# A two-block model on one core: fills of the first attention spread by work, conditioning chunks moved, dense products of the recurrence in halves

## The reference

```python
for l in range(2):
    mod, mod_c = silu(c) @ w_ada[l] + b_ada[l], silu(c_ctx) @ w_ada[l] + b_ada[l]   # 3072 columns: shift, scale, gate
    if l == 0:   # x 512 rows, ctx 256 rows
        q, k, v, g_a, xb, b_g, c_g, g_b = split(modulate(x) @ w_in_ab)        # and the same for ctx
        o_a = window_attention(rope(q), rope(k), v, kc, vc, sink)              # 8 heads, 2 key heads, |s-t| <= 128
        o_b = b_g * short_conv(c_g * xb, conv_w)                               # three taps
        y = concat(o_a * silu(g_a), o_b * silu(g_b)) @ w_out_ab
        x = layer_norm(alpha * x + gate * y); ctx likewise
    else:
        q, zf, zb, i, g = split(modulate(x) @ w_in_c); ctx: zf, zb, i
        # per head and direction: k = 1 - f(z), S_t = diag(f_t) S_{t-1} + k_t v_t, o_t = S_t q_t
        # ctx first gives the starting state; forward and backward are added
        y = (rms(o_f + o_b) * g_norm * silu(g)) @ w_out_c
        x = layer_norm(alpha * x + gate * y)
```

## Time and profile before

| | |
|---|---|
| median of 3 runs | 2454.27 us (2452.99 to 2455.32) |
| profiled execution, its own time | 2457.86 us |
| its span | 2456.1 us |
| mean granted TensorE clock over it | 0.948 |
| first attention's stretch | 209.70 to 463.85 us |
| recurrence's stretch | 609.60 to 1130.80 us |

### The profile page before, as it was taken

The page is one execution under the profiler, slowest core; times in us unless marked ns, Lnnn a source line. Parts: engine busy times, 40 slices in busy tenths (PEclk is TensorE's granted clock), DMA queues, the critical chain, the costliest instruction groups (busy, mean ns, idle before and its releaser), DMA issues. The chain is left out here.

```text
span 2456.1 us, 27907 instructions
## 1 busy us (share of the span) xinstructions
PE 2243.3 (91%) x11655; PEld 1798.7 (73%) x11655; DVE 1104.9 (45%) x1647; ACT 668.0 (27%) x1030; POOL 835.7 (34%) x393
## 2 busy tenths in 40 slices
PE   5989996978999999999798878999998999999998
PEld 3768885856676767787665667888887767888886
DVE  2023557652556556556996553111116783111113
ACT  3222223223444444453111333010003163010111
POOL 1322102410323323223800024554554345454553
PEclk7999997979999999999899988999999999999999
DMA  9321115351101011112121012332322222232322
GB/s 296 83 72 52 35 35 172 79 163 52 35 23 47 18 35 35 35 52 78 42 65 35 35 35 70 102 103 86 103 92 97 86 86 69 86 103 88 101 95 77
DMA packets 173212, 187.45 MB, mean 76 GB/s; under 512 B 25552, under 2 KB 151840, under 8 KB 172960
## 3 DMA queue, kind: packets, MB, share of 16 engines
q1 hardware_dynamic: 165520, 178.56, 23.1%
q10 hardware_dynamic: 6992, 5.01, 0.7%
q0 software_dynamic: 576, 2.10, 0.2%
HBM read 183.56 MB, written 2.10 MB: 76 GB/s over the span
## 5 line engine op out<-in xcount | busy, mean ns | idle before, releaser
L2816 POOL TENSOR_TENSOR weights_lo<-weights_raw,weights_hi 128x2048 fp32r<-128x2048 f32 (+1 forms) x104 | 471.0, 4528 | 849.5 <-ACT weights_hi L1334 637.6
L646 PE MATMUL ring<-input_hi,weights_hi 128*128 128x512 f32 x784 | 305.4, 390 | 0.0
L648 PE MATMUL ring<-input_hi,weights_lo 128*128 128x512 f32 x784 | 305.0, 389 | 0.0
L647 PE MATMUL ring<-input_lo,weights_hi 128*128 128x512 f32 x784 | 305.0, 389 | 0.0
L2653 DVE CAST weights_hi<-weights_raw 128x2048 fp32r<-128x2048 f32 (+1 forms) x72 | 88.8, 1233 | 378.6 <-PE ring L648 173.9
L2807 POOL TENSOR_TENSOR h_w<-h_p 128x512 f32<-128x512 f32 x56 | 70.3, 1256 | 448.1 <-PE ring L935 367.6
L908 PE MATMUL obank<-acts,weights_raw 128*128 128x512 f32 x384 | 175.2, 611 | 0.8 <-issue 0.8
L646 PEld LDWEIGHTS ring<-input_hi,weights_hi 128*128 128x128 f32 x784 | 147.2, 188 | 31.1 <-issue 0.5
L648 PEld LDWEIGHTS ring<-input_hi,weights_lo 128*128 128x128 f32 x784 | 147.2, 188 | 30.6
L647 PEld LDWEIGHTS ring<-input_lo,weights_hi 128*128 128x128 f32 x784 | 147.2, 188 | 30.5 <-issue 0.2
L919 PE MATMUL obank<-weights_raw,acts 128*128 128x256 f32 x640 | 145.4, 387 | 0.0
(11 more groups left out here) (457 smaller groups left out, 4459.2 us busy)
## 6 DMA issues: line engine op xcount, KB each, us to landing
weights_raw<-in_w_ada SPq DMA_DIRECT2D x24, 1024.0 KB, 7.2
weights_raw<-in_ffn_w_gate SPq DMA_DIRECT2D x22, 1024.0 KB, 5.2
weights_raw<-in_ffn_w_up SPq DMA_DIRECT2D x22, 1024.0 KB, 5.2
weights_raw<-in_w_in_c SPq DMA_DIRECT2D x20, 1024.0 KB, 5.1
weights_raw<-in_ffn_w_down SPq DMA_DIRECT2D x16, 1024.0 KB, 4.9
weights_raw<-in_w_in_ab SPq DMA_DIRECT2D x9, 1024.0 KB, 5.2
weights_raw<-in_ev_w_in SPq DMA_DIRECT2D x8, 1024.0 KB, 5.8
weights_raw<-in_od_w_in SPq DMA_DIRECT2D x8, 1024.0 KB, 5.8
```

Source lines behind the costliest of these rows:

```text
L646: pe.matmul(o, hi[:, k, ms], xh[:, k, t0:t0 + n], start=k == 0, stop=False)
L647: pe.matmul(o, hi[:, k, ms], xl[:, k, t0:t0 + n], start=False, stop=False)
L648: last = pe.matmul(o, lo[:, k, ms], xh[:, k, t0:t0 + n], start=False, stop=k == KD - 1)
L2816: pool.tensor_tensor(W_LO[slot][:, 0:kt, :], WR[:, slot, 0:kt, :], w_hi[:, 0:kt, :], ALU.subtract).then_inc(sem("w_lo"), 1)
```

## The change

It does the following, all in the first block.

1. **Fills by work.** A list `a_woven` of all units is spread over 24 even places by cost (`fill_cost`, in matmuls); a place may hold several units.
2. **Conditioning.** Sixteen chunks (`MODS`): five stand behind `kv`, `ga0`, `ga1`, `gb0` and `gb1`, one each; seven are fills; four, (1,8) to (1,11), stand between the first dense products of the recurrence.
3. **Gate rows** of layer 0 are fills; that of layer 1 comes behind the first part of i.
4. **Late high parts.** ScalarE rounds the weights of y0.1 and later at the third tile of the y before it, y0.0 at the unit cg1.1.0, yc0.2 and yc0.3 on either side of LayerNorm's root. Convolution parts run behind the units of cg. x is loaded again from ScalarE's queue in four column pieces.
5. **Turned tiles of layer 1** (`h1.0` to `h1.3`) stand right behind yc0.3, `h1.4` and `h1.5` behind the second part of z. A chunk's slot is given back after its last part, in the order in which chunks were taken.
6. **Recurrence.** Dense products are cut in halves (`product_half`) and spread over the places. The diagonal is made once for a pair of heads, in the backward step, from the sum of both directions' keys (`keys_of_both`). `exclusive` on GpSimd is gone: backward scans on VectorE give the exclusive sums. The first two level operands stand ahead of the diagonal, the query operand behind the first scores.

```diff
-            return units + [None] * (8 - len(units))
+            halves = [unit + (half,) for unit in units for half in range(2)]
+            if st == LAST:
+                share = (2, 2, 2, 2, 2, 0, 0, 0)
+            else:
+                share = (2, 2, 2, 1, 1, 1, 1, 0) if len(units) == 5 else (2, 2, 2, 1, 2, 1, 2, 0)
+            at = [sum(share[:i]) for i in range(9)]
+            return [halves[at[i]:at[i + 1]] for i in range(8)]
...
+        MODS_AHEAD, MODS_LATE = 5, 4
+        a_woven, mods_left = [], list(range(MODS_AHEAD, len(MODS) - MODS_LATE))
+        for nm, c, x, m in AB_UNITS:
+            a_woven.append((nm, c, x, m))
+            if (nm, c, x) == ("cg", 1, 1):
+                a_woven += [("x_again",)] * m + [("y_hi", 2 * m), ("y_hi", 2 * m + 1)]
+            elif (x, m) == (1, 1):
+                a_woven.append(("mod", mods_left.pop(0)))
+            if nm == "bg":
+                a_woven += {(0, 0, 0): [("gate_diag", 0)], (0, 0, 1): [("gate", 0)],
+                            (0, 1, 0): [("gate_diag", 1)], (0, 1, 1): [("gate", 1)]}.get((c, x, m), [])
+        for unit in Y_UNITS[:-3]:
+            a_woven.append(unit)
+            if unit[2] == TL - 1 and mods_left:
+                a_woven.append(("mod", mods_left.pop(0)))
+            if unit == ("y", 2, TL - 1):
+                a_woven += [("ctx_again",), ("last_mod",)]
+        assert not mods_left
+
+        def fill_cost(unit):
+
...
+            return 2 * KD if unit[0] in ("mod", "gate") else 3 * KD * (2 if unit[0] != "y" and unit[2] == 0 else 1)
+
+        A_PLACES = 24
+        a_costs = [fill_cost(u) for u in a_woven]
         AB_FILL = {}
-        for u, unit in enumerate(AB_UNITS):
-            AB_FILL[u * AB_STEPS // len(AB_UNITS)] = unit
-        MOD_FIRST = 6
...
-        Y_WOVEN = 48 - AB_STEPS - MOD_FIRST
-        for u in range(Y_WOVEN):
-            AB_FILL[AB_STEPS + MOD_FIRST + u] = Y_UNITS[u]
-        Y_AFTER = Y_UNITS[Y_WOVEN:]
+        for u, unit in enumerate(a_woven):
+            place = min(A_PLACES - 1, A_PLACES * (2 * sum(a_costs[:u]) + a_costs[u]) // (2 * sum(a_costs)))
+            AB_FILL.setdefault(2 * place, []).append(unit)
         mod_no = {}
...
+            def mod_next(s):
+
+                if s:
+                    mod_turn(*MODS[s - 1])
+                mod_rows(*MODS[s])
+
...
-            mod_run(1, MOD_FIRST, 12)
+            for t in range(TL):
+                pe.wait_ge(sem("x1_ready"), t + 1)
+                turn_tiles("h1.", X, (t,), "va"[t % 2])
...
-            for t in range(6):
-                pe.wait_ge(sem("x1_ready"), t + 1)
-                turn_tiles("h1.", X, (t,), "va"[t % 2])
-            gate_rows(1, 1)
-            pe.wait_ge(*read_of("h1.4"))
-            pe.wait_ge(*read_of("h1.5"))
+            pe.wait_ge(*read_of("h1.2"))
+            pe.wait_ge(*read_of("h1.3"))
...
+            def product_half(unit, half):
+
                 kind, key, part = unit
-                if part == 0:
-                    c_weights[kind, key] = chunk(cols(wc, C_COLS[kind](key)))
+                if half == 0:
+                    if part == 0:
+                        c_weights[kind, key] = chunk(cols(wc, C_COLS[kind](key)))
+                        c_release[kind, key] = len(released)
+                        released.append((None, 0))
+                    n = products[unit] = len(products)
+                    if n >= 2:
+                        pe.wait_ge(sem("products_emptied"), n - 1)
+                n = products[unit]
...
+                if half == 0:
+                    return
                 last.then_inc(sem("products_filled"), 1)
                 if part == C_PARTS[kind] - 1:
-                    released.append((sem("products_filled"), n + 1))
+                    released[c_release[kind, key]] = (sem("products_filled"), n + 1)
...
+            product(("z", 0, 0))
+            mod_rows(1, 8)
+            product(("z", 0, 1))
+            mod_next(13)
+            for t in (4, 5):
+                pe.wait_ge(sem("x1_ready"), t + 1)
+                turn_tiles("h1.", X, (t,), "va"[t % 2])
+            pe.wait_ge(*read_of("h1.4"))
+            pe.wait_ge(*read_of("h1.5"))
+            product(("z", 0, 2))
+            mod_next(14)
+            product(("q", 0, 0))
+            mod_next(15)
+            product(("q", 0, 1))
+            mod_turn(1, 11)
+            product(("i", 0, 0))
+            gate_row(1, 0)
+            product(("i", 0, 1))
...
+                if d:
+                    pe.wait_ge(*product_emptied(("q", hb, 1)))
+                    pe.wait_ge(sem("hg_k_both"), hb + 1)
+                    ps = take(f"dg{st}", "v")
+                    for j in range(TL * HH):
...
+                        last = pe.matmul(ps[:, j * P:(j + 1) * P], HK[0][:, h, ch * P:(ch + 1) * P],
+                                         Q_[:, h, ch * P:(ch + 1) * P], start=True, stop=True)
                     last.then_inc(filled, 1)
                 levels(st, 1)
                 between(1)
...
+                elif unit[0] == "x_again":
+                    act.wait_ge(*fill_of("cg1.11"))
+                    for c in range(4):
+                        cs = slice(c * WC, (c + 1) * WC)
+                        act.dma_start(X[:, 0:TL, cs], a["x"][0][:, cs].rearrange("(t p) n -> p t n", p=P)).then_inc(sem(f"x_again{c}"), 16)
...
+                elif unit[0] == "y":
+                    if unit[2] == 2:
+                        hi_upto(f"y0.{unit[1] + 1}" if unit[1] < 3 else "yc0.0")
+                elif unit[0] == "cg" and unit[1] == 1:
+                    if unit[2:] == (1, 0):
                         hi_upto("y0.0")
...
+            hi_upto("yc0.2")
+            ln_root(1, 0, 4)
+            hi_upto("yc0.3")
+            h1_tile(1)
+            h1_tile(3)
+            ln_root(2, 4, 6)
...
+                else:
+                    if st == 1:
...
+                    for h in range(HH):
+                        dve.tensor_tensor_scan(HP[b][:, h, 1:L], HT_[b][:, h, 0:L - 1], tab("chunk", 1, L), 0.0, ALU.add, ALU.mult)
+                        last = dve.tensor_tensor_scan(HP[b][:, h, L + 1:LT], HT_[b][:, h, L:LT - 1], tab("chunk", 1, LC), 0.0, ALU.add, ALU.mult)
+                    link(last)
+                    link(dve.tensor_tensor(PL[b], ends[0], ends[1], ALU.add))
                 dve.tensor_copy(DEC[b], PL[b]).then_inc(sem("hg_sums"), 1)
 
...
-                idb = IDENT.unsqueeze(1).to_broadcast([P, TL * HH, P])
-                S = HSC[hb % 2]
...
-                    dve.wait_ge(*read_of(f"dg{st}"))
-                else:
-                    dve.tensor_tensor(HDG[:, :, :], src, idb, ALU.mult).then_inc(emptied["v"], 1)
-                    dve.wait_ge(*read_of(f"dg{st}"))
-                    link(dve.tensor_tensor(S[:, :, :], S[:, :, :], HDG[:, :, :], ALU.add))
+                own = IDENT.bitcast(U32).unsqueeze(1).to_broadcast([P, TL * HH, P])
+                dve.copy_predicated(HSC[STEPS[st][0] % 2][:, :, :], own, src).then_inc(emptied["v"], 1)
+                dve.wait_ge(*read_of(f"dg{st}"))
...
+            def keys_of_both(hb):
+
+                k0, k1 = HK[0][:, :, 0:L], HK[1][:, :, 0:L]
+                dve.wait_ge(sem("hg_k"), 2 * hb + 2)
+                dve.tensor_tensor(k0, k0, k1, ALU.add).then_inc(sem("hg_k_both"), 1)
...
+                dve.wait_ge(*product_emptied(("q", hb, 1)))
                 level_operand(7 * st)
-                diagonal(st)
                 level_operand(7 * st + 1)
+                if d:
+                    keys_of_both(hb)
                 level_scores(st, 0)
                 if d == 0 and hb:
                     inside(hb - 1)
+                query_operand(st)
                 states(st)
+                if d:
+                    diagonal(st)
...
-            def exclusive(st):
-
-                b, d = st % 2, STEPS[st][1]
-                if d == 1:
-                    pool.wait_ge(sem("hg_sums"), st + 1)
-                    pool.tensor_tensor(HP[b][:, :, :], HP[b][:, :, :], HT_[b][:, :, :], ALU.subtract).then_inc(sem("hg_excl"), 1)
-                    pool.wait_ge(sem("hg_excl"), STEPS[st][0] + 1)
-
```

257 lines of the change are left out of this document (132 added, 125 removed).

## The result

The changed kernel takes **2429.03 us** (median of 4 runs, 2426.07 to 2432.88) against 2453.78 us of the kernel before in the same series: ratio 0.9887, 95% interval 0.9871 to 0.9903, so about 25 us faster. 2387 us were forecast, with a range of 2362 to 2416. Run again beside the experiments, the same kernel gave a ratio of 0.9865 (0.9849 to 0.988), 2424.47 us. A few executions were slower as a whole, at a lower granted clock; they are left out of every comparison.

A forecast was written before the change was run, and what follows sets the result against it. TensorE was taken to bound the kernel, idle 90 us before the unchanged rest and partly at its low clock. Projections −21, attention −8, tail −18, recurrence −20 gave −67 against 2454.27: 2387 us, range 2362 to 2416.

The forecast's parts named there:

- rival (a): Recurrence: half products starve level 5, so it takes 515 to 520 us; time 2402 to 2440, chance 0.18.
- the three signs of being wrong: Short pairs still wait for a_probs, level 5 waits over 6 us, or PEclk in the recurrence is under 0.93.
- Before the attention: Projections: chunks behind split products and earlier rounding remove waits; 77 us instead of 98.35, −21.
- The attention: First attention: fills spread by work, 227 us content plus new waits and low clock, 246 us in all, −8.
- the short waits of the next scores: Attention: next scores wait 0.34 us for the turn's copy 23 times, 8 us.
- place 34: Attention, ahead of y0.0: late rounding and GpSimd's subtractions make PE wait 6 us, with 3 at the low level behind.
- The tail: Between first attention and recurrence: old waits removed, a new load wait of 7 us; 127 us instead of 145.7, −18.
- The recurrence: Recurrence: diagonal waits and GpSimd's subtraction go, level 5 waits about 4 us in forward steps; 501.5 us, −20.
- The rule weighed against a row: LayerNorm: two GpSimd-VectorE meetings put at 2.7 us each from rows; the skill's rule allows up to 4.6, time 2391.
- (b): Attention and recurrence: PE stays at 2.4 GHz, stretches 235 and 488 us; time below 2372, chance 0.20.
- (c): Up to the recurrence: loads and ScalarE's roundings bound it, gains come back as waits; 2450 to 2458, chance 0.02.
- (d): Recurrence: mixed small matmuls and short waits hold PE at 1.2 GHz, slower, 2481 or 2504 us; chance 0.02.

The follow-up runs named there:

- the narrowed run: Changed kernel with GpSimd's subtractions for y0.0 to y0.3 weights and the attention output's first four tiles cut to a sixteenth or an eighth: 2409.95 us, ratio 0.98.
- late convolution: Changed kernel with VectorE's last two convolution parts moved from ahead of the first joins of y0.0 to behind y0.0: 2428.95 us, ratio 0.986.
- VectorE's low parts: Changed kernel with VectorE instead of GpSimd making the low parts of the attention output's first four tiles: 2425.68 us, ratio 0.9865.
- early rounding: Changed kernel with ScalarE rounding the weights of y0.0 two units earlier, at cg1.0.1, tiles rounded as before: 2428.12 us, ratio 0.9876.
- the same units by number: Changed kernel with its fill units one to a place over 48 places, ahead of and behind the turns: 2431.36 us, ratio 0.9895.
- the shares: Changed kernel with one more half product ahead of level 5 in each forward and backward step of the recurrence: 2408.43 us, ratio 0.98.

## Why the prediction was wrong

The direction was right, and the time fell into the span of rival (a), 2402 to 2440, for its own reasons in part. The range ended at 2416, too low. None of the three signs of being wrong came: no short pair waits for scaled probabilities, level 5 waits 4.56 us, and the recurrence's granted clock is 0.96. What did not fit was the list of waits in the attention: one over 1 us was expected, and there are at least seven. The errors of the four stretches, 1.5, 28.4, 1.9 and 11.1 us, sum to 43 us, where forecast and time are 42 apart. By the steps:

**Before the attention: right.** 77 forecast, 78.51 measured; the clock is 1.00 and no wait is left.

**The attention: wrong by 28 us (20 in the second profile of the same kernel, 265.6), and this is the step that failed: its waits were put at 16 us, with nothing for VectorE being late beside GpSimd.** Its content was right (227; the narrowed run shows 227.5). The forecast's 16 us of waits were 36.5 us (274.35 less 237.81 busy), and its 3 at the low level were 10.8 (237.81 less 227). Term by term: the short waits of the next scores 9.7 instead of 8; the wait ahead of y0.0 7.3 instead of 6; the reload of x cost nothing instead of 2; **12.1 us for VectorE's banks and copies where nothing was put down**, 4.5 where a fill waits for a bank of scores that ScalarE hasn't emptied (3.0, 1.3 and 0.2), and 2.9 behind VectorE's emptying of banks into the convolution's input (a_u: 1.1, 1.0 and 0.8). (One pair gets 80 units of fill, not 72 at most; nothing rests on it.) I had counted GpSimd's subtraction as a delay on its own chain at place 34, and a meeting with VectorE only in the LayerNorm. In the short pairs it meets the joins and the convolution at every y chunk. Narrowing all of it gave 14.5 us, of which I had put down some 9. The runs that moved the meeting instead of taking it away (late convolution, VectorE's low parts, early rounding) gave nothing that could be told from the base. In those whose rows were read (all but the early rounding), the wait that was named shrank and the next join was stretched instead (4.66, 4.05 and 4.82 us, the base's 3.31): there the place isn't bound by the one instruction that a wait names. The rest of the error has other causes: with the subtractions narrow PE is still idle 24.4 us, 14.2 of them ahead of the next scores, put at 8. Why these are longer than 0.34 us each was not tested. The assumption that spreading by work takes away 10.7 + 7.6 + 6.1 us of waits at the price of short ones was also too good: against the same units by number it is worth 7 at most.

**The tail: right.** 127 forecast, 128.95 measured. The wait for (1,10) and q's weights was put at 7 and is 4.92 + 1.18 = 6.1; taking it away shortened the stretch by 8.1.

**The recurrence: mechanism right, size off by 11 us.** 501.5 forecast, 512.64 measured. Level 5 waits 4.56 in three forward steps, put at 4; with 0.85 at level 4 this is 16.2 against 14.4. The chain from 751.68 to level 5's operand is 18.0 us and not 16.4, since scans take 1.94 and 1.46 us beside GpSimd's level operands instead of 1.19 and 0.66. I had taken this surplus off with the four subtractions that are gone; but they ran behind the scans, and it was the level operands that met them before too (VectorE before, step 2):

```profile
783.95 1.22 DVE L2115 TENSOR_TENSOR_SCAN h_p<-tables,h_t 128x512 f32<-128x512 f32 x1
785.09 1.48 DVE L2116 TENSOR_TENSOR_SCAN h_p<-tables,h_t 128x256 f32<-128x256 f32 x1
786.49 1.99 DVE L2115 TENSOR_TENSOR_SCAN h_p<-tables,h_t 128x512 f32<-128x512 f32 x1
```

Backward steps wait 0.30, 0.83 and 1.09, 8.9 in all against 3.2 (four times 0.8), and the low level costs 14 (484 less 470) and not 10. That it was the cover ahead of level 5 the shares show: one more half there made the recurrence 18.8 us shorter.

**The rule weighed against a row.** The Trainium skill, "SBUF — State Buffer", section "Who interferes with whom", has a VectorE instruction with two SBUF inputs contend with a GpSimd instruction that reads SBUF, over ports that one of them holds exclusively, with the order of issue deciding which one is blocked. The trace agrees: the join of 426.70 began 1.2 us behind GpSimd's 425.51 and ended 0.28 behind its end. I had taken 2.7 us for each of the two meetings in the LayerNorm, where the rule gives the rest of GpSimd's 4.6; they cost 2.7 (4.01 instead of 1.28) and 3.7 (4.37 instead of 0.69). In the attention the surplus is 2.8 to 3.2 in the changed kernel's joins (3.21 and 3.60 less 0.42) and 4.2 in the late-convolution run (4.66). The price was near; what was missed is how often it is paid.

**The rivals.** (b) is out: the clock was 0.94 in the attention. (c) is out: the time is 21 us below its span; the attention did keep waiting, mostly for VectorE and for the turn's copy, never for a load; one wait, of 7.3, stands behind the late rounding at place 34. (d) is out: the recurrence's clock is 0.96.

## What to carry to other kernels

Before placing a fill or a rounding, list for each pair what VectorE must do before TensorE goes on, and then which two-input VectorE instructions fall beside a long GpSimd instruction: the named wait shows only the last of them, and in the runs read here moving that one moved part of the wait. Never let a rounded share leave the place ahead of a turn of probabilities empty (40 us slower here, with five such places and smaller fills at others); that all fill should stand there isn't shown, since one unit to a place on both sides cost 7 us at most. When work is taken off an engine, look at which instruction it ran beside before its price is taken off another: here the scans' surplus stayed. In a loop with a chain on other engines, count cover from the point where the chain starts to its use, and give that interval its share first; halves are useful for that, and were badly spent behind the last levels.

## What the runs showed of the hardware

The attention of one and the same program took 265.6 us in one profile and 274.35 in another, with PE idle 34.4 and 36.5 us. The rest of the difference is busy time, 231.21 and 237.81 us at granted clocks of 0.97 and 0.94. The rows of waits differ more than their sum: 8.6 and 12.1 us for VectorE, 11.0 and 9.7 for the turn's copy. Attentions that differ by less than that can't be ranked by one profile's length. VectorE's scans are stretched beside GpSimd too, though less than its arithmetic: the scan of 763.07 took 1.94 us instead of 1.19, and GpSimd's instruction that began during it, at 763.89, took 1.95 instead of 1.04; neither waited for the other's end.
